# Twelve of the attention's eighteen modulation jobs made inside the delta rule's scan

## The reference

```python
def second_block(x, c, ctx, c_ctx, mod_w, mod_b, ...):
    sc, scc = silu(c), silu(c_ctx)
    for i in range(DEPTH):                      # DEPTH = 2
        m = (sc @ mod_w[i] + mod_b[i]).reshape(B, 6, 1, D)      # mod_w[i]: 1024 x 6144
        mc = (scc @ mod_w[i] + mod_b[i]).reshape(6, D)
        h = rmsnorm(x, norm1_g[i]) * (1 + m[:, 1]) + m[:, 0]
        ...                                     # attention (i = 0) or recurrent scan (i = 1)
        x = x + m[:, 2] * y
        h2 = rmsnorm(x, norm2_g[i]) * (1 + m[:, 4]) + m[:, 3]
        x = x + m[:, 5] * swiglu(h2)
```

```python
u, w = triangular_solve(lmat, [v * beta, k * beta * exp(gc)])   # lmat from k @ k.T and the decays
v_new = u - w @ s
o = (q * exp(g)) @ s + aqk @ v_new
s = s * exp(glast) + (k * exp(glast - g)).T @ v_new
```

## Time and profile before

| | |
|---|---|
| Median of 3 runs | 4130.4 us (4124.05 to 4132.95) |
| The profiled execution | 4123.75 us, of it 4122.5 us in the profile's span |
| TensorE busy | 3700.5 us (90%), granted clock 0.936 |
| VectorE, ScalarE, GpSimd busy | 1657.6 us (40%), 1191.1 us (29%), 1377.5 us (33%) |
| Chain that ended last | TensorE 72%, ScalarE 8%, VectorE 6%, GpSimd 5%, DMA 2% |
| Loads | 263.76 MB, mean 64 GB/s |

### The profile page before, as it was taken

One profiled execution on the slowest core, in us unless ns is written; L12 is line 12 of the kernel. 1 busy time (PEld: TensorE's weight loads), 2 busy tenths in 40 slices (PEclk: granted clock), 3 DMA queues, 4 the chain that ended last, 5 costly groups with the idle time before them and its releaser, 6 DMA issues.

```text
span 4122.5 us, 72507 instructions
## 1 busy us (share of the span) xinstructions
PE 3700.5 (90%) x31840; PEld 2364.9 (57%) x31840; DVE 1657.6 (40%) x2926; ACT 1191.1 (29%) x2160; POOL 1377.5 (33%) x1214
## 2 busy tenths in 40 slices
PE   7998778999898988889899999898788888889998
PEld 3755565434444455555455555354566666748887
DVE  1344343223444122444433233532655555533334
ACT  3253222221212174432300000201555565520001
POOL 1320442011212112656432323351543343425444
PEclk9998687988999999989999999999899999989999
DMA  5420000521101211540111111222000000022222
GB/s 194 146 94 21 2 1 11 205 84 33 33 23 51 82 46 64 178 158 21 51 56 57 62 61 52 97 81 77 3 16 15 28 15 15 14 82 82 92 82 72
DMA packets 196131, 263.76 MB, mean 64 GB/s; under 512 B 6087, under 2 KB 151495, under 8 KB 193640
## 3 DMA queue, kind: packets, MB, share of 16 engines
q1 hardware_dynamic: 188880, 242.78, 17.6%
q10 hardware_dynamic: 6936, 16.35, 1.0%
HBM read 246.52 MB, written 12.58 MB: 63 GB/s over the span
## 4 chain that ended last, share of the span: by engine, by line
PE 72%; ACT 8%; DVE 6%; issue 6%; POOL 5%; DMA 2%; SPq 0%; ACTq 0%; DVEq 0%; POOLq 0%
PE ps L236 57%; PE ps L2943 2%; PE ps L759 2%; PE ps L484 1%; ACT mem L836 1%; PE ps L1959 1%; PE ps L786 1%; POOL mem L2846 1%; PE ps L774 1%; PE ps L378 1%; DMA mem<-rkv 1%; DVE mem L1159 1%; PE ps L493 1%; PE ps L1277 1%; DVE mem L817 1%
## 5 line engine op out<-in xcount | busy, mean ns | idle before, releaser
L236 PE MATMUL ps<-mem 64*64 64x64 f32 (+6 forms) x25344 | 2744.1, 304 | 203.2 <-ACT mem L661 35.9
L236 PEld LDWEIGHTS ps<-mem 64*64 64x64 f32 (+1 forms) x25344 | 1779.6, 156 | 1179.5 <-issue 606.0
L2846 POOL TENSOR_TENSOR mem<-mem 128x256 f32<-128x256 f32 (+1 forms) x264 | 238.5, 920 | 356.7 <-ACT mem L3301 185.3
L854 POOL TENSOR_SCALAR mem<-mem 128x768 f32<-128x768 f32 (+2 forms) x128 | 219.2, 1725 | 199.4 <-DVE mem L820 199.3
L2141 ACT ACTIVATE mem<-ps 128x384 f32<-128x384 f32 (+1 forms) x80 | 35.7, 446 | 838.8 <-PE ps L236 788.3
L2128 POOL TENSOR_TENSOR mem<-mem 128x512 f32<-128x512 f32 (+1 forms) x80 | 100.1, 1251 | 440.9 <-PE ps L236 392.2
L2152 DVE TENSOR_TENSOR mem<-mem,ps 128x384 f32<-128x384 f32 (+1 forms) x80 | 39.9, 499 | 442.9 <-PE ps L236 442.9
L2943 PE MATMUL ps<-mem 128*128 128x128 f32 x960 | 180.5, 307 | 32.3 <-DVE mem L2868 21.4
L591 POOL TENSOR_TENSOR mem<-mem 128x512 f32<-128x512 f32 (+1 forms) x72 | 74.7, 1062 | 393.3 <-ACT mem L586 391.6
L2876 ACT ACTIVATE mem<-ps 128x256 f32<-128x256 f32 (+1 forms) x220 | 101.5, 461 | 198.7 <-PE ps L2943 198.5
L2868 DVE TENSOR_TENSOR mem<-mem,ps 128x256 f32<-128x256 f32 (+1 forms) x220 | 109.5, 513 | 116.7 <-PE ps L236 116.1
(11 more groups left out here) (326 smaller groups left out, 4049.1 us busy)
## 6 DMA issues: line engine op xcount, KB each, us to landing
mem<-i_mod_w SPq DMA_DIRECT2D x48, 1024.0 KB, 6.8
mem<-i_ffn_wg SPq DMA_DIRECT2D x22, 1024.0 KB, 5.1
mem<-i_ffn_wu SPq DMA_DIRECT2D x22, 1024.0 KB, 5.2
mem<-i_e_w_in SPq DMA_DIRECT2D x16, 1024.0 KB, 6.0
mem<-i_o_w_in SPq DMA_DIRECT2D x16, 1024.0 KB, 5.6
mem<-i_ffn_wd SPq DMA_DIRECT2D x16, 1024.0 KB, 5.3
mem<-i_e_mod_w SPq DMA_DIRECT2D x12, 1024.0 KB, 6.0
mem<-i_o_mod_w SPq DMA_DIRECT2D x12, 1024.0 KB, 7.3
```

Source lines behind the costliest of these rows:

```text
L236: ins = e.h.matmul(out, l, r, start=(i == 0), stop=(i == n - 1))
L854: K.pool.h.tensor_scalar(w, w, stat(i, o, 1), None, MUL).then_inc(*nm.up(tag, i, o))
L2846: K.pool.h.tensor_tensor(m3(self.slot(l)), self.lraw, bm(C(K, f"cm{self.d}", l, 64), 2 * self.np), MUL).then_inc(*self.mk.up(key, l))
```

## The change

In the scan a mod_stream of twelve jobs (mod_b0 24 to 48, mod_b1 0 to 24) runs as a fourth stream, on TensorE and VectorE, with banks 6 and 7, with one row buffer of its own, and with a ring of its own, made of the two slots of the weight ring that are free there. A new generator, between, gives each of its 13 steps a place: the end of step 4 of lane 0's unit and of lane 1's (8 or 7 steps apart), when neither chain has a product. SP waits for the fence, then loads the 24 slabs in order; the two loads of the z columns follow and wait for the last job's products. In the attention six jobs stay (mod_b1 24 to 48). mod_stream takes the row buffers as an argument; with one, the copy of job i waits for the turning of job i-1. Four small arrays of delta_gates are now allocated behind delta_inputs, above the mark that is taken back for the scan.

```diff
@@ mod_stream
-def mod_stream(K, banks, bq, jobs, ring=None):
+def mod_stream(K, banks, bq, jobs, ring=None, rows=None):
...
-    ring = ring or K.ring
+    ring, rows = ring or K.ring, rows or K.rows
...
-                    ins = K.pe.h.matmul(K.ps[bq][:, 2 * j:2 * j + 2], K.rows[q % 2][:, j * 128:(j + 1) * 128], C(K, "sel"), start=True, stop=True)
+                    ins = K.pe.h.matmul(K.ps[bq][:, 2 * j:2 * j + 2], rows[q % len(rows)][:, j * 128:(j + 1) * 128], C(K, "sel"), start=True, stop=True)
...
-                if i >= 2:
-                    K.dve.wait_ge(*turn.at(*jobs[i - 2]))
-                K.dve.h.tensor_copy(K.rows[i % 2], K.ps[bank(i)]).then_inc(*row.up(n, m))
+                if i >= len(rows):
+                    K.dve.wait_ge(*turn.at(*jobs[i - len(rows)]))
+                K.dve.h.tensor_copy(rows[i % len(rows)], K.ps[bank(i)]).then_inc(*row.up(n, m))
@@ deltanet
-    G, BE, AB, T1, T2 = K.a3(6, 8), K.a3(6, 8), K.a3(6, 16), K.a3(6, 8), K.a3(6, 8)
-    ea = K.alloc(8)
+    G, BE = K.a3(6, 8), K.a3(6, 8)
...
+    AB, T1, T2, ea = K.a3(6, 16), K.a3(6, 8), K.a3(6, 8), K.alloc(8)
@@ delta_scan
+    jobs = mod_jobs(("mod_b0", 24, 48), ("mod_b1", 0, 24))
+    ring = Ring(K, "mslab", [K.ring.slots[K.ring.slot(first + i)] for i in range(2)], "dn")
...
+    m_pe, m_dve, m_sp = mod_stream(K, (6,), 7, jobs, ring, [K.alloc(512)])
...
-    for unit, chain, z in ((unit_pe, chain_pe, z_pe), (unit_dve, chain_dve, z_dve), (unit_act, chain_act, z_act), (unit_pool, chain_pool, z_pool)):
-        run(lane(unit, chain, 0), lane(unit, chain, 1), later(8 + 6 * 17, z()))
+    def between(g):
+        for j in range(2 * 7):
+            for _ in range(7 if j % 2 else 8 if j else 4):
+                yield
+            if next(g, 0) == 0:
+                return
+            yield
+    run(lane(unit_pe, chain_pe, 0), lane(unit_pe, chain_pe, 1), later(8 + 6 * 17, z_pe()), between(m_pe()))
+    run(lane(unit_dve, chain_dve, 0), lane(unit_dve, chain_dve, 1), later(8 + 6 * 17, z_dve()), between(m_dve()))
+    run(lane(unit_act, chain_act, 0), lane(unit_act, chain_act, 1), later(8 + 6 * 17, z_act()))
+    run(lane(unit_pool, chain_pool, 0), lane(unit_pool, chain_pool, 1), later(8 + 6 * 17, z_pool()))
+    K.settle(K.sp)
+    run(m_sp())
+    for i, m in enumerate(ring.spent_at[n] for n in (2 * len(jobs) - 2, 2 * len(jobs) - 1)):
+        K.ring.spent_at[first + i - 3] = K.ring.spent_at[first + i - 3] + m
@@ attention
-    mod_pe, mod_dve, mod_sp = mod_stream(K, (7,), 7, mod_jobs(("mod_b0", 24, 48), ("mod_b1", 0, 48)))
+    mod_pe, mod_dve, mod_sp = mod_stream(K, (7,), 7, mod_jobs(("mod_b1", 24, 48)))
```

## The result

The change makes the kernel slower: median 4138.2 us against 4122.0 of the kernel before on the same chip (20 runs each), ratio 1.0036 with a 95% interval of 1.0023 to 1.0049, so about 15 us. Forecast was +26.4. The profiled execution took 4135.76 us (span 4134.5), 12.0 more than before. By stretches of the two traces, scan +31.0, attention -20.3 (282.20 to 261.88), all the rest +1.3. That rest is -5.8 ahead of the scan and +7.1 behind it, in stretches that the change doesn't touch: in one pair of profiles a stretch can differ by so much without a cause in the kernel.

What follows compares the result with a forecast made beforehand. TensorE bounds the scan's passes at the low clock level, about half with engine hand-overs at the high one. Scan +41.9, VectorE +3.6, attention -19.1 gave +26.4 us: 4157 us, range 4128 to 4176.

Steps and rivals of the forecast that it cites:

- (1) Attention: Attention blocks 3 to 6 lose their jobs and become like the last two; blocks 1 and 2 unchanged: 19.07 us less.
- (2) TensorE in the scan: Scan: ten batch places at low clock cost 3.64 us each, two at 2.74, no gain behind: +41.9 us.
- bounds for this: Scan, most gain from a returned clock level, per place: pass 1.46 us shorter, wide products 2.57 us shorter.
- Rows 7: Kernel's start: batches and small products from 26.57 to 33.73 stay at low-level durations; by these a job costs 5.37 us.
- (3) VectorE: Scan: row copy waits for small products and holds up VectorE's later work, 0.3 us a job: +3.6 us.
- (4) Loads: Scan: the 24 slab loads and the later z-column loads are hidden behind other work: 0 us.
- B: Scan's low clock level stays through batch and small products: +43.7 us, 4174 us; chance 0.22.
- C: Scan: batch brings the high level back, held through pass and wide products: -13.9 us, 4116.5 us; chance 0.10.
- D: Scan: TensorE's idle time takes in half the batches' time: +5.5 us, 4136 us; chance 0.12.
- E: Scan: slabs come late at several places, each wait holding both lanes: 4198 us; chance 0.04.
- the scan's 343 us and its clock of 0.74: Scan from first product to dense tail at 343 us, clock near 0.74; wrong if growth under 25 or over 60 us.
- The sign that I had set for a mis-sized attention: Attention: the forecast is wrong if it shrinks by less than 15 or more than 24 us.

Runs made afterwards that it cites:

- e1: The attention's part of the change alone, the twelve jobs made nowhere and the scan as before: ratio 0.9934 to the kernel before, -27 us.
- e2: The scan's part alone: the change with all eighteen jobs still in the attention, twelve made twice: ratio 1.0091 to the kernel before, +37.5 us.
- e5: The kernel before plus eight unused products, as wide as a job's, at each of the change's places in the scan: ratio 1.0018, 7 us slower.
- e6: The kernel before plus eight unused narrow products (128 x 128 weights, 2 columns) at each of the change's places: ratio 1.0096, 40 us slower.
- e10: The change with the small products of the job before put ahead of each batch, not behind it: ratio 1.0036 to the kernel before.
- e13: The change with all eighteen jobs kept in the attention, without the scan's 24 loads (a constant replaces the slabs): ratio 1.0077 to the kernel before.
- e8: The change with batches ahead of a 2.3 us TensorE wait, in banks free before it, small products at step 7: ratio 0.9923 to the kernel before.
- e9: The kernel before plus eight unused wide products and four narrow ones behind them at each of the change's places: ratio 1.0055.
- e12: The kernel before plus eight unused wide products per place, in bank 7 ahead of product t, where TensorE waits some 2.3 us: ratio 0.9995.
- e3: The change with the small products and addition moved from behind the batch to step 7, where TensorE waits 0.55 us: ratio 0.9983 to the kernel before.

## Why the prediction was right or wrong

**The direction and the bound** were right: the batches went to places where TensorE is busy, and cost more than the attention gave. The size was not, +26.4 against about +15. Two terms of the sum were mis-sized: the attention's, and the gain behind a batch in the scan, which I took as zero. By the parts measured alone, -27 for -19.1 and +37.5 for +45.5, each is off by about 8 us. Neither ratio's interval leaves the forecast out (18 to 36 and 28 to 48 us); for the attention fourteen profiles do.

**(1) Attention**, -19.1. The pair of profiles seems to confirm it (blocks 3 to 6 gave 141.05 - 122.25 = 18.8 us, the whole stretch 20.3), but that was luck: e1's median says 27 us, and so do seven profiles with eighteen jobs against seven with six (27.2). The step that failed is "Jobs 1 to 6 stay in the first two blocks (77.31 us, unchanged)". By the trace before, seven batches run in blocks 1 and 2 (112 records of L484) and eleven in blocks 3 to 6 (176), and those first two blocks take 76.2 to 80.0 us with eighteen jobs in the stretch and 70.1 to 75.3 with six. Blocks 3 to 6 differ by 20.4 us on the mean of the same profiles, near the 19.1. What the first two blocks gain beyond the one batch of 1.9 us isn't explained by a run; the granted clock of the whole stretch is .91 to .93 with eighteen jobs and .93 to .96 with six, so the level takes part in it.

**(2) TensorE in the scan**, +41.9. The price of a batch was right: its level does return inside it, as I let it, 2.73 us on average from start to next instruction over twelve batches (the sign was 2.7), and the small products 1.05 us. Those two make 45 us. The step that failed is "and no gain after it, because the pass behind it is sparse work and loses the level again, as it does now". It loses it again, but later: L1308 behind the batch still ran at the high level in 8 of 12 places and the last transposes in 7 of 11, and only by the wide products was the level gone in nine of twelve. Till then the pass's own products were shorter, by 20.3 us against before's scan and by 8.4 against e1's (e2's by 2.9). That a wide batch gives such a gain is shown by e5 and e6 (148.3 and 189.5 us for the same instructions); its size in the change is known only as 3 to 20 us. I had bounds for this (1.46 and 2.57 us a place) and took zero of them. The page TensorE: Matmul & The Clock Gate of the Trainium skill, Part 1, says that activity releases the throttle, and the batches' durations agree (2.75 us, between 3.64 and 1.92); it spoke for a gain of some size. Rows 7, which I set against it, show batches and small products in turn and a level that stays low; after e6 and e10 I read that row as one on small products in between (1.86 and 3.64 us there too), not on batches alone, which no run tests apart.

**(3) VectorE**, 3.6: 3.8 by the rows. **(4) Loads**, 0: right (e13), with no wait of L484 on a slab in the scan of the change (idle 0.0 in its group).

**The rivals.** B is out at 2.73 us a batch and 1.05 us for the small products behind it; with narrow products in place of the batch its mechanism exists (e6). C's mechanism was at work for a part, its clock of over 0.8 was measured (.81, though e1's scan has .80 without a job), and e5 shows it nearly whole: it wins in ten of eleven places when no small products follow. D is out for this place, since the waits grew; it is right for another one (e8). E is out.

**The signs.** Blocks of 30.6 us, the batch's 2.7 us, the copy's wait for L493 and the longer wait ahead of L1308 came as told (0.82 us rather than 0.5); the scan's 343 us and its clock of 0.74 did not (328, 0.81). The sign that I had set for a mis-sized attention, more than 24 us, isn't met by the pair's 20.3 us and is met by the 27 us of the other runs.

**Open:** how large the gain behind the batches of the change is, between 3 and 20 us; why the attention gains 27 us and not some 21; why L1280 is high in some passes of one kernel and low in others, with the same rows ahead; the share of copies and additions beyond the rows' 3.8 us; and the part of e9's scan time that its median doesn't show.

## What to carry to other kernels

Look for the wait, not for the step at which a chain is idle by the program's order: the same twelve jobs cost 37 us among dense products and nothing that could be measured in a wait of 2.3 us, once they had a bank that was free before it. When wide work is put into a stretch at TensorE's low level, price the stretch behind it too: its own products get shorter, and rows at both levels give the bounds. And keep small products away from such a batch; put them where TensorE waits anyway. Last, don't take a term as confirmed because one pair of profiles agrees with it: here six other profiles of the attention with six jobs were all shorter than the change's.

## What was not expected of the hardware

Useless wide work can be nearly free: 34.7 us of it cost 7 us (e5), 29.9 us cost nothing measurable (e12), since the instructions behind ran at the high level (42 us shorter in e5's seven groups than before, 30 than in e1). Products of 128 x 128 weights and 2 columns, 38.5 us of them without a pause inside each group, cost all of their time, and the granted clock stayed at 0.73. Yet the same kind of products, put into a wait of 0.55 us while the level was high, went together with a level that held through the wide products behind in ten of eleven places (e3).
